# All eight slices of gate and up as split products, one low half made by GpSimd

## The reference, cut to what matters

```python
def swiglu(h, wg, wu, wd):
    return (jax.nn.silu(h @ wg) * (h @ wu)) @ wd

def run_block(args):                       # one block of tokens that chose expert e
    tok, wt, e = args
    y = swiglu(h_pad[tok], w_eg[e], w_eu[e], w_ed[e])
    return y * wt[:, None].astype(y.dtype)
...
routed = jax.ops.segment_sum(y_blocks.reshape(n_pad, d), tok_buf, num_segments=t + 1)[:t]
return routed + swiglu(h, w_sg, w_su, w_sd)
```

## Time and profile before

| What | Value |
|---|---|
| median of 3 runs | 2325.89 us (2323.56 to 2327.89) |
| the profiled execution | 2333.98 us, span 2332.3 us, mean granted TensorE clock 0.955 |
| TensorE busy | 2035.9 us, 87% of the span |
| VectorE, ScalarE, GpSimd busy | 1432.4, 1278.9, 869.0 us |
| first and last scatter of the expert loop issued | 1231.4 and 2271.5 us |
| `w_low` on VectorE, 318 operations | 378.2 us, 1217 ns each |
| plain gate/up matmuls, 420 records | 197.1 us busy |

### The profile page before, as it was taken

The page is one execution under the profiler, slowest core; times in us unless marked ns, Lnnn a source line. Parts: engine busy times, 40 slices in busy tenths (PEclk is TensorE's granted clock), DMA queues, the critical chain, the costliest instruction groups (busy, mean ns, idle before and its releaser), DMA issues. The chain is left out here.

```text
span 2332.3 us, 35734 instructions
## 1 busy us (share of the span) xinstructions
PE 2035.9 (87%) x9400; PEld 1452.3 (62%) x9401; DVE 1432.4 (61%) x2085; ACT 1278.9 (55%) x2004; POOL 869.0 (37%) x876
## 2 busy tenths in 40 slices
PE   4999995889888887899839999999999999999980
PEld 2776673655555554666427777777766777777760
DVE  3751564663358433455537777777676777777773
ACT  2421122556666565222127777776766777777761
POOL 1010103631155110044434455555444545544561
PEclk8999997899999998999969999999999999999995
DMA  6464436411221111343289998789999888789736
GB/s 248 140 190 118 130 115 187 114 32 39 44 48 39 39 35 63 133 92 101 56 255 293 317 336 247 231 233 328 336 330 331 260 232 229 203 258 334 202 61 233
DMA packets 284779, 420.25 MB, mean 180 GB/s; under 512 B 27233, under 2 KB 213345, under 8 KB 284689
## 3 DMA queue, kind: packets, MB, share of 16 engines
q1 hardware_dynamic: 213314, 281.25, 35.2%
q0 software_dynamic: 60496, 116.37, 22.6%
q10 hardware_dynamic: 10896, 21.71, 3.0%
HBM read 352.51 MB, written 91.54 MB: 190 GB/s over the span
## 5 line engine op out<-in xcount | busy, mean ns | idle before, releaser
L1802 DVE TENSOR_TENSOR w_gate_up_low<-w_gate_up,w_gate_up_high 128x1024 fp32r<-128x1024 f32 x318 | 378.2, 1217 | 15.9 <-ACT w_gate_up_high L1747 15.9
L1831 DVE TENSOR_TENSOR w_down_low<-w_down,w_down_high 128x2048 fp32r<-128x2048 f32 x104 | 238.4, 2292 | 161.5 <-ACT w_down_high L1771 161.5
L1747 ACT ACTIVATE w_gate_up_high<-w_gate_up 128x1024 fp32r x318 | 312.1, 1047 | 39.4 <-issue 28.6
L935 DVE TENSOR_REDUCE neg_max<-ps_scores 128x1 f32<-128x1280 f32 x128 | 190.3, 1490 | 223.6 <-PE ps_scores L1020 223.2
L1876 PE MATMUL ps_gu<-w_gate_up_high,gatheredT_high 128*128 128x512 f32 x630 | 256.1, 407 | 2.7 <-DVE gatheredT_low L1810 1.4
L1878 PE MATMUL ps_gu<-w_gate_up_high,gatheredT_low 128*128 128x512 f32 x630 | 248.7, 395 | 0.0
L1877 PE MATMUL ps_gu<-w_gate_up_low,gatheredT_high 128*128 128x512 f32 x630 | 248.6, 395 | 0.0
L1695 POOL DMA_INDIRECT gathered<-h_scratch,e_gather_index x108 | 195.6, 1811 | 96.5 <-POOL e_gather_index L1692 91.2
L1709 POOL DMA_INDIRECT y_scratch<-e_y,e_target_index x104 | 182.5, 1754 | 95.3 <-ACT e_y L1784 39.0
L1771 ACT ACTIVATE w_down_high<-w_down 128x2048 fp32r x104 | 199.6, 1919 | 29.2 <-issue 28.0
L1020 PE MATMUL ps_scores<-k_high_low,q_high 128*128 128x512 f32 (+1 forms) x384 | 167.5, 436 | 47.0 <-ACT probs L895 18.9
(11 more groups left out here) (257 smaller groups left out, 4328.9 us busy)
## 6 DMA issues: line engine op xcount, KB each, us to landing
w_gate_up<-in_w_exp_gate SPq DMA_DIRECT2D x64, 1024.0 KB, 10.4
w_gate_up<-in_w_exp_up SPq DMA_DIRECT2D x64, 1024.0 KB, 13.9
w_down<-in_w_exp_down SPq DMA_DIRECT2D x64, 1024.0 KB, 15.5
w_mod_later<-in_w_mod ACTq DMA_DIRECT2D x32, 512.0 KB, 3.8
w_mod_first<-in_w_mod SPq DMA_DIRECT2D x4, 2048.0 KB, 15.6
w_in_raw<-in_w_in SPq DMA_DIRECT2D x32, 256.0 KB, 3.9
k_high_low<-k_scratch POOLq DMA_DIRECT2D x10, 640.0 KB, 8.0
values<-in_tokens SPq DMA_DIRECT2D x10, 512.0 KB, 11.3
```

The lines of the kernel that those rows point to most:

```text
L935: nc.vector.tensor_reduce(nm[:, n % 4:n % 4 + 1], S[:, span(u, r)], AX.X, ALU.max, negate=True).then_inc(s_m, 1)
L1747: act.activation(wH[:, 2 * j:2 * j + 2], wgu[:, ds(slot, 1), 2 * j:2 * j + 2].rearrange("p o k n -> p (o k) n"), ACT.Copy).then_inc(S["wH" ...
L1802: nc.vector.tensor_tensor(wL[:, 2 * j:2 * j + 2], wgu[:, ds(slot, 1), 2 * j:2 * j + 2].rearrange("p o k n -> p (o k) n"), wH[:, 2 * j:2 * ...
L1831: nc.vector.tensor_tensor(dl[:], wdn[:, ds(slot, 1)].rearrange("p o k n -> p (o k) n"), dh[:].bitcast(F32), ALU.subtract).then_inc(S["dl"], 1)
```

## The change

`SPLIT` goes from 6 to 8: there is no plain product left, and gate and up are 24 split matmuls in four pairs of slices. `xN` and its copy on ScalarE go; `xH`, `xL`, `wH`, `wL` get two more slices. ScalarE makes a fourth high half of the weights, which waits for the end of the gate/up product of the block in front (`gu`). The low half of the last pair is made by GpSimd (`w_low_last`), in its body between the index load and the scatter; TensorE waits for its new semaphore `wLp` ahead of the last pair. The copy of the target numbers moves ahead of the wait for the landing of the scatter in front, and this wait now stands directly at the scatter. The loop over the two halves of y on ScalarE is written differently and does the same.

```diff
-SPLIT = 6
+SPLIT = 8
...
+            def w_low_last(n):
+                slot = read(pool, 2, n, WS - 1)
+                pool.wait_ge(S["wH"], n * NS + NS)
+                pool.sem_inc(S["carry"], 1)
+                j = NS - 1
+                nc.gpsimd.tensor_tensor(wL[:, 2 * j:2 * j + 2], wgu[:, ds(slot, 1), 2 * j:2 * j + 2].rearrange("p o k n -> p (o k) n"),
+                                        wH[:, 2 * j:2 * j + 2].bitcast(F32), ALU.subtract).then_inc(S["wLp"], 1)
+
             def body(i, n, u):
                 gather(n + 4, i + 2, u)
                 index(n + 6, u)
-
+                w_low_last(n + 2)
+
+                nc.gpsimd.tensor_copy(si[u][:], ir[:, ds(n & (RING - 1), 1)]).then_inc(S["target"], 1)
+                pool.wait_ge(S["target"], n + 1)
+                pool.wait_ge(S["y"], n * 2 + 4)
                 pool.wait_ge(S["scat"], n * 16 + 32)
-                pool.sem_inc(S["carry"], 1)
-                nc.gpsimd.tensor_copy(si[u][:], ir[:, ds(n & (RING - 1), 1)]).then_inc(S["target"], 1)
-
-                pool.wait_ge(S["y"], n * 2 + 4)
-                pool.wait_ge(S["target"], n + 1)
                 pool.sem_inc(S["carry"], 1)
...
+            w_low_last(0)
             gather(2, 1, 0)
             gather(3, 1, 1)
+            w_low_last(1)
             turns = blocks(pool, body)
...
                 for j in range(NS):
-                    if not head:
-                        act.wait_ge(S["wused"], n * NS + (j + 1 - NS))
+                    if not head and j < NS - 1:
+                        act.wait_ge(S["wused"], n * (NS - 1) + (j + 2 - NS))
+                    if not head and j == NS - 1:
+                        act.wait_ge(S["gu"], n)
...
-                    if k1 < 4 * g + 4:
-                        act.activation(xN[:, k1 - SPLIT:4 * g + 4 - SPLIT], src[:, k1 - 4 * g:], ACT.Copy)
...
                 x_low(n + 2)
-                w_low(n + 2, slot, range(1, NS))
+                w_low(n + 2, slot, range(1, NS - 1))
...
                 for j in range(NS):
-                    pe.wait_ge(S["wL"], n * NS + (j + 1))
+                    if j < NS - 1:
+                        pe.wait_ge(S["wL"], n * (NS - 1) + (j + 1))
+                    else:
+                        pe.wait_ge(S["wLp"], n + 1)
...
-                for k in range(SPLIT, KD):
-                    last = nc.tensor.matmul(psG[:], xN[:, k - SPLIT], wgu[:, ds(slot, 1), k].rearrange("p o n -> p (o n)"),
-                                            start=False, stop=(k == KD - 1))
```

More of the change, by code:

```diff
@@ L1620, in experts @@
         xL = b.sb(ph, "gatheredT_low", [P, SPLIT, P], F32R)
-        xN = b.sb(ph, "gatheredT", [P, KD - SPLIT, P])
         wH = b.sb(ph, "w_gate_up_high", [P, SPLIT, 2 * FE], F32R)
@@ L1641, in experts @@
             "xT", "xH", "xL", "wH", "wL", "wused", "gu", "silu", "act", "aTp", "aH", "dh", "dl",
-            "dn", "y", "weight", "rows", "target", "scat", "landed", "carry", "zeroed")}
+            "dn", "y", "weight", "rows", "target", "wLp", "scat", "landed", "carry", "zeroed")}
         s_gather = [b.sem(ph, f"e_gathered{u}") for u in range(2)]
@@ L1780, in body @@
                 act.wait_ge(S["scat"], n * 16 + 16)
[L1781 to L1784, removed]
+                for h in range(2):
+                    act.wait_ge(S["dn"], n * 2 + (2 + h))
+                    act.activation(yb[u][:, h * 512:(h + 1) * 512], psY[:, h], ACT.Copy).then_inc(S["y"], 1)
             act.sem_inc(S["y"], 2)
@@ L1841, in body @@
                 x_low(n + 2)
-                w_low(n + 2, slot, range(1, NS))
-            w_low(0, ring(0), range(NS))
+                w_low(n + 2, slot, range(1, NS - 1))
+            w_low(0, ring(0), range(NS - 1))
             x_low(0)
@@ L1851, in _ @@
             x_low(1)
-            w_low(1, slot, range(1, NS))
+            w_low(1, slot, range(1, NS - 1))
             blocks(dve, body)
@@ L1878, in gate_up @@
                         last = nc.tensor.matmul(psG[:], xL[:, k], wH[:, k], start=False, stop=(k == KD - 1))
-                    last.then_inc(S["wused"], 1)
-                for k in range(SPLIT, KD):
-                    last = nc.tensor.matmul(psG[:], xN[:, k - SPLIT], wgu[:, ds(slot, 1), k].rearrange("p o n -> p (o n)"),
-                                            start=False, stop=(k == KD - 1))
+                    if j < NS - 1:
+                        last.then_inc(S["wused"], 1)
                 last.then_inc(S["gu"], 1)
```

## The result

The changed kernel takes 2564.93 us in the median of 4 runs (2553.73 to 2571.13), the kernel before 2326.89 beside it: a ratio of 1.102, 95% interval 1.0995 to 1.1048. The sign of the forecast was right, the size was not: +238 us where +49 was forecast, and outside the range.

What follows compares the result with a forecast made beforehand. Bounds: TensorE in quick stretches (9.7 us a block), the scatter ring elsewhere (10.45). VectorE's 10.4 and a slower 10.65 added 57 x 0.7 = +40 and 47 x 0.2 = +9: +49 us, 2375 us, range 2305 to 2445.

Steps and rivals of the forecast that it cites:

- GpSimd's chain: GpSimd's work from one scatter issue through gather, index, subtraction, copy and start-up: 9.5 us, 7.9 with a short gather.
- VectorE's round of 10.4 us: VectorE's block in the expert loop: 7.72 us busy plus a 2.34 us hold by GpSimd's subtraction, gaps and jitter.
- TensorE's gain of 0.35 us a block: Gate/up: six split matmuls (1.36 us) replace the plain slices (1.71 us), making TensorE's own round 9.35 us.
- 2.34 us forecast: Duration of GpSimd's new 128x1024 subtraction, scaled from a 128x1280 one of 2.93 us; bounds 2.3 to 2.7.
- The subtraction 2.34, copy 0.18 and start-up 0.90: Last terms of GpSimd's block, behind 5.92 us to the index load's end and a 0.15 us table read: 9.5 us.
- So it is ready near 1.8, starts at 2.3: GpSimd's subtraction, in us after gate/up starts: ready after a 1.06 us gather, then held by w_low, ending at 4.65.
- rival C: GpSimd ready after down_low begins: waits 2.2 us, round 11.8 or more; 2503 us, 2439 for half the blocks; chance 0.25.
- cost 0, hidden behind TensorE: ScalarE's extra high half less one x copy: busy 8.3 us a block, under 9.35; 0.8 us if uncovered.
- The target copy ahead: Copy before the landing wait: 0.3 us a block off the scatter ring, from 10.1 to 9.8, start-up staying behind.
- D: Rival: new copy order does nothing, scatter ring stays 10.45 in slower stretches; 2389 us, chance counted within the forecast's 0.50.
- TensorE's idle time before the last pair: Sign: TensorE waits 0.5 to 1 us a block for GpSimd's low half; over 2 us would make the prediction wrong.
- its signs: Prediction wrong if VectorE's records keep their lengths, quick rounds stay under 9.8 us, or the last pair waits over 2 us.

Runs made afterwards that it cites:

- all-VectorE kernel with the high half moved: Changed kernel with all low halves of the weights on VectorE and ScalarE's fourth high half behind silu and x_high: 2302.02 us, ratio 0.989; without that move 2335.67 us.
- copy-only one: Kernel before, six split slices, with only the target copy moved ahead of the wait for the scatter's landing: 2304.64 us, ratio 0.988.
- kernel with the copy first: Changed kernel with GpSimd copying the target numbers before its subtraction instead of behind it: 2448.73 us, ratio 1.050.

## Why the prediction was wrong

The mechanism, that a VectorE operation with two SBUF inputs and a GpSimd operation that reads SBUF exclude each other, was named and priced for one operation only. The step that failed is GpSimd's chain: the copy behind the subtraction was put at 0.18 us and took 1.90, and the subtraction was put 2.3 us behind the start of gate/up and began 3.2 us behind it in the median. By that GpSimd's chain, and not VectorE's round of 10.4 us, set the undisturbed block, and the late subtractions came on top. Step by step:

- TensorE's gain of 0.35 us a block: the matmuls were as forecast, and the gain had no bound to act on. It shows in stretches of the all-VectorE kernel with the high half moved. There a block has 46 matmuls (24, 8, 12, 2), so the one below, with TensorE busy throughout, runs at 9.35 us a block, as worked out. Over the whole run little of it is left: that kernel takes 2302 us, and the copy-only one with its plain slices 2305.

```profile
1300.00:1350.00 50.00, 50.00 (x246) 41.61 (x245) 47.27 (x54) 43.67 (x57) 25.46 (x26) 1.00 1.06 347
```

- The subtraction: 2.34 us forecast, 2.41 in the median (2344 ns minimum). Right.
- "The subtraction 2.34, copy 0.18 and start-up 0.90": this term failed, and it is the largest error in the undisturbed round, 11.58 us for 9.5. The copy took 1.90 us in the mean, 2.24 in the median, because it queued behind a down_low that the subtraction itself had held up. The exclusion was applied to the subtraction and to down_low, and not to the next reader of SBUF behind it, though the earlier trace rows had the gather at 2.62 us under down_low, which the prediction used for one rival. The kernel before also has copies held in this way. The one below waited out the down_low that ran from 1512.60 to 1514.89, and the target copy, 184 ns in the median, reached 2262. Moving the copy ahead was worth 116 us, late subtractions and start-up included.

```profile
1512.05 2.87 POOL L1692 COPY e_gather_index<-e_index_ring 128x1 uint32 x1
```

- "So it is ready near 1.8, starts at 2.3": this failed too. The subtraction starts 3.2 us after the product's first matmul in the median, and later than 3.0 us, the bound that rival C named, in 57 of 104 blocks. One reason is the gather, put at the 1.06 us of the earlier trace rows. In the kernel before it took 1676 ns in the median and under 1.2 us in 43 of 108; in the changed kernel it did so in 4 of 108.
- The chance that down_low begins first was put into a rival (0.25) and left out of the forecast. It happened in 30 of 104 rounds, and the late subtractions cost some 86 us with what followed from them. The forecast worked out one order of two operations that start 0.05 to 0.14 us apart in the rounds shown; such a race should have been priced as both.
- ScalarE, "cost 0, hidden behind TensorE": wrong. Its busy time is covered, but the new high half waits for the end of the product and stands ahead of silu and x_high. It costs 34 us in the kernel that isolates it; in the changed kernel it wasn't measured alone. The wait was in the diff; what was queued behind it wasn't counted.
- The target copy ahead: 0.3 us of the ring forecast, 0.49 in the rounds shown. D fell: the half of the change that was forecast as a gain is one (25 us), but in the changed kernel nothing waits for the landing, so nothing of it is left.
- VectorE's round of 10.3 to 10.4 us was near (10.8 in the kernel with the copy first), but in the changed kernel it wasn't the longest: GpSimd's was.
- TensorE's idle time before the last pair, forecast as 0.5 to 1 us a block, is 176.9/104 = 1.7. In the mean that is under the 2 us at which the prediction called itself wrong, and VectorE's records did lengthen, so none of its signs spoke clearly; none of them looked at the copy. Rival C had the right picture, and its half-way time, 2439, is still 126 us short; it had the copy at 0.18 as well.
- The exclusion in the SBUF — State Buffer page of the Trainium skill (Who interferes with whom) is borne out: both lengthen with a subtraction (2.29 to 3.53 us), and neither with a write (2.31). What the page infers of a DMA's descriptors beside a tensor_tensor isn't: the scatter's issue took 3.09 us under down_low for 1.65. That operation reads its row numbers from SBUF too, and no run separates the two.

## What to carry to other kernels

An operation moved to GpSimd costs its own time, what it holds up on VectorE, and what the held-up VectorE operation then holds up on GpSimd; list every SBUF reader behind it in its queue, not the operation alone. Where it must be, let it run beside VectorE's work on PSUM and early enough for the engine that needs it: one place or the other was worth 196 us here for the same work. Read from the trace what it then meets, since the same place in the list met w_low once ScalarE's order changed, and 37 us were lost again. And a new wait is priced by what stands behind it in its engine's order, even on an engine with time to spare.

## What the runs showed of the hardware that I had not expected

- GpSimd's copy of one number for each partition waits out a whole VectorE operation of two SBUF inputs: 2.24 us for 0.18. The issue of an indirect scatter does so as well, 3492 ns in the median for 1647, in the kernel with the copy first.
- A GpSimd memset, 2.29 us in the mean, runs beside VectorE's operations of two SBUF inputs: down_low stays at 2309 ns and w_low at 1217.
- Some start-up of an indirect DMA comes after its last wait, whatever that wait is for: 0.80 us behind a landing, 0.86 to 0.92 behind a copy or y, and 1.07 or 1.08 ahead of the scatter in the changed kernel.
- The scatter lands sooner in the changed kernel, 6.5 us for 8.8, with the DMA share at 0.73 to 0.80 for 0.84 to 0.96. It isn't the longer round alone: in the kernel with the copy first, at 11.18 us a block, the landing takes 9.0 us, of which the longer issue is a part. The runs don't say what the cause is.
